# Loading all cached keys as 32x32 squares and turning them on VectorE

## The reference, cut to what matters

```
q, k, v = sb_qkv(x, w_in)                                   # x (8, 16, 1024)
k_all = concatenate([k_cache, k], axis=1)                   # k_cache (8, 1024, 16, 64), float32
z = einsum('bqhd,bkhd->bhqk', q, k_all) * SB_SCALE
log_keep = where(mask, log_sigmoid(-z), 0)
after = cumsum(log_keep, axis=3, reverse=True) - log_keep
w = where(mask, exp(log_sigmoid(z) + after), 0)
o = einsum('bhqk,bkhd->bqhd', w, v_all)
```

## Time and profile before

| What | Value |
|---|---|
| median of the runs | 2436.64 us |
| profiled execution, its own time | 2434.27 us |
| its span, first to last instruction | 2432.5 us |
| mean granted TensorE clock, share of 2.4 GHz | 0.998 |
| PE busy | 2412.1 us (99%) |
| DVE busy | 1651.7 us (68%) |
| ACT busy | 1102.0 us (45%) |
| DMA packets | 377091, 259.16 MB |
| one pair of heads in the middle of the attention stage | 46.8 us |

### The profile page before, as it was taken

How to read it: one execution, slowest core, us unless ns; L and a number is a source line. 1 busy time by engine, 2 the same in 40 slices (tenths; PEclk the granted TensorE clock), 3 DMA queues, 4 the chain that set the end, 5 groups by cost and what they waited for, 6 DMA issues and landing times.

```text
span 2432.5 us, 38883 instructions
## 1 busy us (share of the span) xinstructions
PE 2412.1 (99%) x15460; PEld 2168.7 (89%) x15460; DVE 1651.7 (68%) x2168; ACT 1102.0 (45%) x1779; POOL 450.0 (18%) x386
## 2 busy tenths in 40 slices
PE   9999999999999999999999999999999999999998
PEld 8999999999999998999999988777776899999987
DVE  7766667886766676876667653666666885676667
ACT  5433344354433344643334433666665443344343
POOL 3221113221121100121112101212223321121100
PEclk9999999999999999999999999999999999999999
DMA  4322232223222232132222225777876132222231
GB/s 139 113 78 73 84 93 90 62 80 111 88 77 74 83 106 88 56 114 74 87 87 87 90 80 157 212 199 203 229 200 195 44 113 87 87 87 80 79 104 70
DMA packets 377091, 259.16 MB, mean 107 GB/s; under 512 B 10385, under 2 KB 339089, under 8 KB 376912
## 3 DMA queue, kind: packets, MB, share of 16 engines
q1 hardware_dynamic: 371808, 239.64, 34.0%
q0 software_dynamic: 5104, 17.04, 2.2%
HBM read 248.22 MB, written 8.42 MB: 106 GB/s over the span
## 4 chain that ended last, share of the span: by engine, by line
PE 95%; DVE 2%; ACT 1%; issue 1%; DMA 0%; POOL 0%; SPq 0%; DVEq 0%; ACTq 0%
PE ps L2749 85%; PE ps L826 6%; PE ps L858 2%; PE ps L2798 2%; PE ps L935 1%; DVE x L2132 0%; ACT wt L1734 0%; DMA x<-in_x_sample_dram 0%; ACT e_buf L1709 0%; ACT kc_t L1693 0%; PE ps L849 0%; DVE e_buf L2454 0%; DVE small L2073 0%; DVE x L2141 0%; DMA raw<-in_ffn_w_dram 0%
## 5 line engine op out<-in xcount | busy, mean ns | idle before, releaser
L2749 PE MATMUL ps<-xt_hi,ring 128*128 128x320 f32 (+2 forms) x3328 | 782.2, 310 | 0.9 <-DVE tmp L2264 0.4
L2749 PEld LDWEIGHTS ps<-xt_hi,ring 128*128 128x128 f32 x3328 | 569.1, 188 | 11.5 <-issue 8.4
L2749 PE MATMUL ps<-ring,h_hi 128*128 128x512 f32 x1760 | 551.5, 390 | 0.0
L2026 DVE TENSOR_TENSOR ring<-raw,ring 128x1024 fp32r<-128x1024 f32 (+1 forms) x317 | 432.1, 1369 | 125.9 <-ACT ring L1432 125.4
L2749 PE MATMUL ps<-xt_lo,ring 128*128 128x320 f32 (+2 forms) x1664 | 514.1, 309 | 0.0
L2749 PE MATMUL ps<-s_ops,ring 128*128 128x320 f32 x3168 | 505.9, 309 | 0.0
L2749 PEld LDWEIGHTS ps<-s_ops,ring 128*128 128x128 f32 x3168 | 474.7, 188 | 0.8 <-issue 0.8
L2749 PEld LDWEIGHTS ps<-ring,h_hi 128*128 128x128 f32 x1760 | 330.4, 188 | 69.3 <-DVE x L2115 0.8
L1432 ACT ACTIVATE ring<-raw 128x1024 fp32r<-128x1024 f32 (+1 forms) x317 | 285.9, 931 | 229.9 <-PE ps L2749 211.8
L1213 POOL TENSOR_TENSOR t_buf<-raw,t_buf 128x512 f32<-128x512 f32 x88 | 115.1, 1308 | 1330.9 <-DVE t_buf L2068 1330.9
L2749 PE MATMUL ps<-ring,h_lo 128*128 128x512 f32 x880 | 343.1, 390 | 0.0
(11 more groups left out here) (210 smaller groups left out, 2504.9 us busy)
## 6 DMA issues: line engine op xcount, KB each, us to landing
raw<-in_ffn_w_dram SPq DMA_DIRECT2D x263, 512.0 KB, 4.1
k_raw<-in_cache_k_dram SPq DMA_DIRECT2D x128, 256.0 KB, 5.1
v_raw<-in_cache_v_dram SPq DMA_DIRECT2D x128, 256.0 KB, 4.2
raw<-in_sb_w_in_dram SPq DMA_DIRECT2D x24, 512.0 KB, 5.3
raw<-in_ple_w_gate_dram SPq DMA_DIRECT2D x16, 512.0 KB, 4.0
g_b<-in_ln_g_dram POOLq DMA_DIRECT2D x8, 512.0 KB, 5.8
b_b<-in_ln_b_dram POOLq DMA_DIRECT2D x8, 512.0 KB, 7.7
raw<-in_sb_w_out_dram SPq DMA_DIRECT2D x8, 512.0 KB, 5.4
```

What stands on the lines that cost most here:

```text
L2026: ve.tensor_tensor(ring[:, slot, 1, col:col + cols], conversion_source(u), ring[:, slot, 0, col:col + cols].bitcast(F32), ALU.subtract).th ...
L2749: return pe.matmul(out, w, xx, start=first, stop=last, skip_group_check=True)
```

## The change

SP loads the keys as 32 partitions x 16 blocks x 32 columns, four DMAs for each stream j (one for each group of 32 features), so 16 a sample in place of 4, with runs of 128 bytes. Partition r of a group gets key 32m+r. DVE's stream transpose turns each 32x32 square in place of its partitions and columns and writes `kc_t` directly, 128 x 1024 an instruction, two a sample (`turned`). PE's transposes, the "kT" events and the copies of ACT and DVE from PSUM go. `scores` waits for `keys_turned`. DVE's `turned` waits for all 16 DMAs of the sample and for PE's scores of the sample before, which read the same `kc_t`. SP's `load_keys` waits for `keys_turned` of sample s-2. The copies of `own_sp` and `q_blk` go from DVE to ACT.

```diff
@@ STEP_EVENTS: all ("kT", su, j) entries go, for instance
-    3: [("kT", 1, 2), ("kT", 1, 3)],
-    8: [("kT", 3, 0), ("kT", 3, 1), ("kB",), ("kT", 3, 2), ("kT", 3, 3)],
+    8: [("kB",)],
...
-        kc = cache_k[0].rearrange("b (k p) h d -> p b k (h d)", p=P)
+        kc_blocks = cache_k[0].rearrange("b (m r) h d -> r b m (h d)", r=BLOCK)
...
-            def cached_keys(i, key):
-                _, su, j = key
-                sample = 4 * i + su
-                pe.wait_ge(k_loaded[sample % 2], 64 * (sample // 2) + 64)
-                bank = event_bank((i, key))
-                for kb in range(SB):
-                    ins = pe.transpose(ps[:, bank, kb * P:(kb + 1) * P], k_raw[:, sample % 2, j, kb, :], ident)
-                ins.then_inc(aux_full, 1)
...
@@ scores
-                for j in range(SB):
-                    pe.wait_ge(*evacuated((i, ("kT", su, j))))
+                pe.wait_ge(keys_turned, 2 * (4 * i + su + 1))
...
@@ load_keys
                 for j in range(SB):
                     if sample >= 2:
-                        sp.wait_ge(aux_full, event_at[(sample - 2) // 4, ("kT", (sample - 2) % 4, j)][0] + 1)
-                    sp.dma_start(k_raw[:, slot, j], kc[:, batch + j, blocks, i * P:(i + 1) * P]).then_inc(k_loaded[slot], 16)
+                        sp.wait_ge(keys_turned, 2 * (sample - 2) + j // 2 + 1)
+                    for q in range(P // BLOCK):
+                        col = i * P + q * BLOCK
+                        dst = k_raw[q * BLOCK:(q + 1) * BLOCK, slot, j].rearrange("p k n -> p (k n)")
+                        sp.dma_start(dst.rearrange("p (m c) -> p m c", c=BLOCK),
+                                     kc_blocks[:, batch + j, first:first + SB * P // BLOCK, col:col + BLOCK]
+                                     ).then_inc(k_blocks_loaded[slot], 16)
...
@@ ACT gets own_softplus (after softplus_hi of units 0 and 1) and sample_queries (after ("qB",)), loses turned
+                def own_softplus(i, u):
+                    g = NU * i + u
+                    se.wait_ge(sp_done, g + 1)
+                    se.activation(own_sp[:, :, u, :], e_buf[:, g % 2, 0:P].rearrange("p (b s) -> p b s", s=DEC_SEQ),
+                                  ACT.Copy).then_inc(own_copied, 1)
...
@@ DVE
+                    if g >= 2 and (g - 2) % NU < 2:
+                        ve.wait_ge(own_copied, 2 * ((g - 2) // NU) + (g - 2) % NU + 1)
...
                 def turned(i, su, half):
-                    evacuate_event((i, ("kT", su, 2 * half + 1)))
+                    sample = 4 * i + su
+                    ve.wait_ge(k_blocks_loaded[sample % 2], 16 * (P // BLOCK) * SB * (sample // 2 + 1))
+                    if sample == 0:
+                        ve.wait_ge(v_full, 2 * TILES)
+                    else:
+                        ve.wait_ge(z_full, NU * ((sample - 1) // 4) + SAMPLE_AT[(sample - 1) % 4] + 1)
+                    two = slice(2 * half, 2 * half + 2)
+                    ve.transpose(kc_t[:, two].rearrange("p j k n -> p (j k n)"),
+                                 k_raw[:, sample % 2, two].rearrange("p j k n -> p (j k n)")).then_inc(keys_turned, 1)
```

More of the change, by code:

```diff
@@ L77 @@
 CAUSAL = [unit for unit in UNITS if unit[0] == "p"]
+BLOCK = 32
 STEP_EVENTS = {
-    0: [("kT", 0, 2), ("kT", 0, 3)],
     1: [("qA",)],
-    2: [("kT", 1, 0), ("kT", 1, 1), ("tot",)],
-    3: [("kT", 1, 2), ("kT", 1, 3)],
+    2: [("tot",)],
     4: [("qB",), ("past",)],
-    5: [("kT", 2, 0), ("kT", 2, 1)],
-    6: [("kT", 2, 2), ("kT", 2, 3)],
     7: [("kA",)],
-    8: [("kT", 3, 0), ("kT", 3, 1), ("kB",), ("kT", 3, 2), ("kT", 3, 3)],
-    9: [("kT", 0, 0), ("kT", 0, 1), ("kt4",), ("kt1",)],
+    8: [("kB",)],
+    9: [("kt4",), ("kt1",)],
 }
@@ L97, in event_on_act @@
 def event_on_act(event):
-    return event[2] % 2 == 0 if event[0] == "kT" else event[0] in ON_ACT
+    return event[0] in ON_ACT
 def events_of(i, u):
@@ L499, in streaming_trunk @@
         last_lo_done = sem("last_lo_done")
-        k_loaded = [sem("k_loaded0"), sem("k_loaded1")]
+        k_blocks_loaded = [sem("k_blocks_loaded0"), sem("k_blocks_loaded1")]
+        keys_turned = sem("keys_turned")
         v_loaded = [sem("v_loaded0"), sem("v_loaded1")]
@@ L968, in values @@
                 ins.then_inc(pv_done, 2)
-            def turn_keys(i, su, half):
-                for j in (2 * half, 2 * half + 1):
-                    cached_keys(i, ("kT", su, j))
             for name in OF_NEXT[0:4]:
                 project(0, (name,))
-            turn_keys(0, 0, 0)
             keys_to_tokens(0, ("kt4",))
@@ L984, in attend @@
                 scores(i, 0)
-                turn_keys(i, 0, 1)
                 if i:
@@ L1007, in attend @@
                     scores(i, 3)
-                    turn_keys(i, 1, 1)
                 else:
@@ L1011, in attend @@
                     values(i - 1, 9)
-                    cached_keys(i, ("kT", 1, 2))
                 suffix(i, 1)
-                if not follows:
-                    cached_keys(i, ("kT", 1, 3))
-                elif i:
+                if follows and i:
                     values(i - 1, 9)
@@ L1030, in attend @@
                 suffix(i, 3, (0, 1) if follows else (0,))
[L1031 to L1034, removed]
+                if not follows:
                     suffix(i, 3, (1,))
-                    cached_keys(i, ("kT", 2, 1))
                 scores(i, 6)
-                turn_keys(i, 2, 1)
                 suffix(i, 4)
@@ L1132, in load_keys @@
                 batch, blocks = sample_slices(su)
+                first = blocks.start * P // BLOCK
                 for j in range(SB):
                     if sample >= 2:
-                        sp.wait_ge(aux_full, event_at[(sample - 2) // 4, ("kT", (sample - 2) % 4, j)][0] + 1)
-                    sp.dma_start(k_raw[:, slot, j], kc[:, batch + j, blocks, i * P:(i + 1) * P]).then_inc(k_loaded[slot], 16)
+                        sp.wait_ge(keys_turned, 2 * (sample - 2) + j // 2 + 1)
[5 more added lines that the diff above has]
+                                     ).then_inc(k_blocks_loaded[slot], 16)
             def load_values(sample):
@@ L1691, in evacuate_event @@
                 se.wait_ge(aux_full, k + 1)
-                if name == "kT":
-                    se.activation(kc_t[:, event[2]], src.rearrange("p (t n) -> p t n", n=P), ACT.Copy).then_inc(aux_free_act, 1)
-                elif name == "kt4":
+                if name == "kt4":
                     se.activation(k_tok[:, :, :], src.rearrange("p (t n) -> p t n", n=P),
@@ L1719, in softplus_hi, with sample_queries @@
                     se.activation(sp_hi[:, h, at:at + n], e_buf[:, g % 2, 0:n], ACT.Copy).then_inc(sp_hi_done, 1)
+                def own_softplus(i, u):
[3 more added lines that the diff above has]
+                                  ACT.Copy).then_inc(own_copied, 1)
+                def sample_queries(i):
+                    if i == 0:
+                        se.wait_ge(q_blk_zero, 2)
+                    se.wait_ge(*evacuated((i, ("qB",))))
+                    for h in range(2):
+                        rows = slice(HEAD_DIM * h, HEAD_DIM * (h + 1))
+                        se.activation(q_blk[i % 2][rows, :, h, :], q_t[i % 2][rows, SEQ:].rearrange("p (b s) -> p b s", s=DEC_SEQ),
+                                      ACT.Copy).then_inc(q_blk_done, 1)
                 def sample_rows(i, u):
@@ L1739, in split_o @@
                     se.activation(o_parts(0, c), o_source(c), ACT.Copy).then_inc(last_hi_done, 1)
-                def turned(i, su, half):
-                    evacuate_event((i, ("kT", su, 2 * half)))
                 def save_prompt(i):
@@ L1761, in attend_act @@
                     if name == "qB":
+                        sample_queries(0)
                         cvt_to(first_qk + QK_SLOTS + 1)
-                turned(0, 0, 0)
                 evacuate_event((0, ("kt4",)))
@@ L1768, in attend_act @@
                     last = not follows
-                    turned(i, 0, 1)
                     if i:
@@ L1776, in attend_act @@
                     softplus_hi(i, 0)
+                    own_softplus(i, 0)
                     if i:
@@ L1781, in attend_act @@
                     softplus_hi(i, 1)
+                    own_softplus(i, 1)
                     if follows:
@@ L1787, in attend_act @@
                     if i == 0 or last:
-                        turned(i, 1, 0)
-                    if i == 0 or last:
                         weights(g)
@@ L1792, in attend_act @@
                     if 0 < i < PAIRS - 1:
-                        turned(i, 1, 0)
                         weights(g)
-                    if i == 0:
-                        turned(i, 1, 1)
                     exp_ln(g + 3)
@@ L1800, in attend_act @@
                         save_samples(i - 1)
-                    elif i:
-                        turned(i, 1, 1)
                     weights(g + 1)
-                    if last:
-                        turned(i, 1, 1)
```

(17 more changed lines are left out.)

8 lines of the change are left out of this document (removed).

## The result

| | Before | After |
|---|---|---|
| median of the runs, us | 2436.66 | 2493.23 (2491.27 to 2493.8) |
| ratio, 95% interval | | 1.0232 (1.0219 to 1.0244) |
| span of the profiled execution, us | 2432.5 | 2492.1 |
| mean granted TensorE clock | 0.998 | 0.975 |

The account below looks back on a forecast made before the run. PE bound the kernel at 46.8 us a pair; after the change DMA would, at 52.3. The +5.5 us times eight pairs, +44, takes the profiled 2434.3 to 2478 us, 2481 as median; range 2410 to 2650.

Parts of the forecast that it names:

- PE, -7.0 us a pair: Attention stage, PE: 64 key transposes a pair go, 46.8 to 39.8 us a pair with nothing in the way.
- DVE and ACT: Attention stage: DVE 30.9 to 34.3 us a pair (stream transpose 1.35 us), ACT 31.0 to 27.4; both hidden, nothing gained or lost.
- The packet, 14.7 ns: Key loads: a 128-byte packet costs 9.5 ns fixed plus 5.2 for bytes, from a line through larger packets; keys 30.1 us.
- Rivals 3 and 4: Key packets: 3, a byte costs twice, 2550 us, chance 0.20; 4, any packet costs 29.6 ns, 2684 us, chance 0.13.
- rival 1: Key packets cheap, up to 13.5 ns: DMA keeps the old pace or better, likelier 2400 to 2430 us, chance 0.17.
- the 52.3 that I took as the period: Attention stage, DMA engine time a pair: 21.7 us rest, 30.1 keys, 0.5 semaphore packets; taken as the pair's period.
- the overlap that I hadn't granted: DMA queue: a never-empty queue shows 106.6% as packets overlap, so 52.3 us could pass in 49.1; not granted in full.
- the estimate of 10.9 ns: Key loads: gentler price of a 128-byte packet, 7/19 of a 512-byte one, from about 3 cycles overhead plus one per 32 bytes.
- SP, 41.4 us, "this alone stops nobody": SP queue: 82 issues a pair at 0.505 us, below 46.8; values and weights 6 us later each time, delaying nobody.
- The sign that I had given for the engines: Attention stage: the DMA share should read about 1.0 in slices where it was 0.7 to 0.8.
- The sum, +44 us: Whole stage: a pair grows from 46.8 to 52.3 us, +5.5, times eight pairs; 2481 us as median.
- The clock (rival 5): Attention stage, PE: idle time lowers its clock, 62 us of PE work a pair, +122 us, 2558 us, chance 0.05.

## Why the prediction was right, and where its sizes were off

The direction holds, and so does the mechanism in the main. PE's saving was hidden under key loads, and the wait showed where it was put, at DVE's stream transposes.

- *PE, -7.0 us a pair.* With the loads out of the way the pair fell by 5.6 us (46.8 to 41.2). The term was a quarter too large, since other waits come up when PE gets shorter.
- *DVE and ACT.* 1.24 us for a stream transpose, not 1.35, and 0.3 us for a small copy on ACT. Both stayed under the pair's length; the position of the small copies is worth nothing in the two runs that test it.
- *The packet, 14.7 ns.* Measured 14.2 ns in the changed kernel by the share of queue 1. The line through larger packets carried down to 128 bytes. Its fixed part of 9.5 ns could have been checked beforehand: the packets of 4 bytes that DMAs post for their semaphores take 10.4 ns on average in the trace of the kernel before (1600 to 1800 us). Rivals 3 and 4 fall with it; rival 1 fails too, but by little, 14.2 ns against its 13.5. With the engines as the only limit a pair took 51.9 us, close to the 52.3 that I took as the period. That is partly luck: a packet costs more in a full queue (15.8 ns), and the overlap that I hadn't granted gives about as much back. The Trainium skill, "DMA: Bandwidth & Descriptors", section "Why small descriptors are slow (HBM only)", led to the estimate of 10.9 ns, which is too low here; the estimate took in the 3 cycles alone, and not the descriptor bytes that the section names as a second cost. The same page of the Trainium skill, section "Specifications", asks for at least 512 bytes for line rate, and the stage agrees in that it moved 177 GB/s in place of 205. That the engine would read, modify and write, which rival 3 priced as a byte that costs twice, no run here shows.
- *SP, 41.4 us, "this alone stops nobody".* This is the step that failed. As a sum it is below the period, but issues and packets don't overlap freely. Where keys are issued one after the other, they come 0.53 us apart, slower than the engines take them (512 x 14.2 / 16 = 0.45 us); where values are in the queue it pushes back and SP can't run ahead. So the pace is SP's in one phase and the engines' in the next, and the pair takes 55.5 us where 51.9 would do. With long runs, as many issues and as few partitions cost 32.5 us over the run. The sign that I had given for the engines, a DMA share of about 1.0, didn't come either: queue 1 read 87.7%. I also missed that PE would wait for values behind 16 key issues; putting them first moved the wait to the keys.
- *The sum, +44 us.* The eight pairs give seven periods. The first five grew from 46.8 to 55.5 us, 8.7 each in place of the 5.5 forecast. The last two are other pairs than I had counted: before the change PE had less work in them, with fewer projections for a next pair, while the key and value loads are the same.

```profile
1797.83 0.44 PE L876 MATMUL ps<-ident_r,o_past 128*128 128x128 f32 x2
...
1838.54 0.38 PE L876 MATMUL ps<-ident_r,o_past 128*128 128x128 f32 x2
...
1875.34 0.38 PE L876 MATMUL ps<-ident_r,o_past 128*128 128x128 f32 x2
```

The same after the change, from 1839.88 us on:

```profile
1896.51 0.63 PE L866 MATMUL ps<-ident_r,o_past 128*128 128x128 f32 x2
...
1934.65 0.38 PE L866 MATMUL ps<-ident_r,o_past 128*128 128x128 f32 x2
```

The sixth period grew from 40.7 to 56.6 us, nearly as much as two of the others, and the seventh from 36.8 to 38.1, as the loads end in it (the last key DMA is issued at 1906.9 us). Together 5 x 8.7 + 15.9 + 1.3 = 60.7 us, which is the 59.6 us between the two profiled executions within about a microsecond; the medians differ by 56.6. That eight times 5.5 came near it is in part luck.
- *The clock (rival 5).* It did fall, to 0.83 in mid-stage, so my argument that short idle spells speak against it did not hold. The rival's +122 us did not come; what the lower clock costs by itself stays open within the bound above.

What stays open: how much the 32 partitions of a key DMA add, in the runs with short and with long runs of bytes alike. No run wrote short runs to 128 partitions, or long ones in 16 DMAs to all 128.

## What to carry to other kernels

Before moving a transpose off PE by loading data in smaller squares, count packets as well as bytes: here four times the packets made a load of the same bytes cost twice the engine time, in a stage whose DMA share was already 0.79. Add the issues: the queue that issues and the engines that move are each a limit, and where their phases alternate neither hides the other in full: 55.5 us a pair here, where the engines alone take 51.9 and the issues alone some 44 (an estimate, 64 x 0.53 + 18 x 0.55). A share of the work moved, as much as the DMA engines can feed, gave a gain where moving all of it gave a loss.

## What the runs showed that I had not expected

- A key DMA of 512 packets of 128 bytes is issued every 0.53 us; one of 128 packets of 512 bytes and the same 64 KB every 0.475 us (medians over the stage). Making packets fewer hardly helped the issuing queue; making DMAs fewer did (51.9 us a pair in place of 55.5).
- The small packet's price is not low because it is small: 14.2 ns for 128 bytes against 29.6 ns for 512, so nearly half the price for a quarter of the bytes. It is not a constant either: 13.9 ns on average in a queue that reads 87.7%, 15.8 ns in one that reads 104.3%.
- A lead in loads can hide an overrun for several pairs: the kernel with two samples on DVE ran 44.3 us a pair at first and 47.3 later, so a window early in a stage would have given the wrong pace.
